# Hybrid diffusion step on one Trainium2 core: recurrence and mixing merged into one block, with the gate-bias wait placed later

## What is computed

```
h   = rmsnorm(x) * (1 + scale1) + shift1                 # modulation from SiLU(c) @ ada_w + ada_b
p   = h @ w_in + b_in                                    # q, k, v, o, 16 gates, 512 Fourier columns
C_loc, n_loc = sum_l w_l v_l k_l^T, sum_l w_l k_l        # per 128-row chunk, 4 heads, 2 directions
C_new = a C + bb C_loc                                   # scan over the chunks: the states
hm  = normalised (intra-chunk part + C_s q), both directions, * head_g * sigmoid(o)
fu  = real(fftn(u)) over (grid rows, grid columns, channels)
x   = x + gate1 * (concat(hm, fu) @ w_out)
h   = rmsnorm(x) ...; x = x + gate2 * ExpertChoiceMoE(h) # 16 experts
```

## Time and profile before

| | us |
|---|---|
| median of 3 runs | 2373.26 (2371.6 to 2374.95) |
| the profiled execution | 2370.94 |
| its span, first to last instruction | 2369.1 |
| input projection, TensorE's first to last L463 | 32.1 to 427.3 |
| recurrence block, SP's first transfer | 437.4 |
| mixing block, SP's first transfer | 519.3 |
| first output product (L1215) | 553.3 |
| first transfer of the expert weights | 766.2 |

### The profile page before, as it was taken

How to read it: one execution, slowest core, us unless ns; L and a number is a source line. 1 busy time by engine, 2 the same in 40 slices (tenths; PEclk the granted TensorE clock), 3 DMA queues, 4 the chain that set the end, 5 groups by cost and what they waited for, 6 DMA issues and landing times. The chain is left out here.

```text
span 2369.1 us, 37037 instructions
## 1 busy us (share of the span) xinstructions
PE 2186.1 (92%) x15013; PEld 1890.2 (80%) x15013; DVE 489.5 (21%) x1246; ACT 358.7 (15%) x1012; POOL 270.0 (11%) x266
## 2 busy tenths in 40 slices
PE   5999999868997299999999999999999999999992
PEld 1445454655553299999999999999999999999992
DVE  0111114247764610011111100110111010101102
ACT  0111112323231011101111111011111110111102
POOL 0000000011211102021021120220210202202102
PEclk8999999999999599999999999999999999999996
DMA  9531010245331777797986976978979769779775
GB/s 377 227 130 62 31 62 22 94 149 200 131 109 58 220 263 213 253 353 222 315 280 238 364 219 246 363 220 294 304 231 355 232 246 363 219 275 327 225 257 178
DMA packets 351601, 528.76 MB, mean 223 GB/s; under 512 B 12996, under 2 KB 292284, under 8 KB 348232
## 3 DMA queue, kind: packets, MB, share of 16 engines
q1 hardware_dynamic: 336456, 509.35, 62.1%
q0 software_dynamic: 15104, 18.88, 3.8%
HBM read 492.23 MB, written 35.95 MB: 223 GB/s over the span
## 5 line engine op out<-in xcount | busy, mean ns | idle before, releaser
L1626 PE MATMUL ps_ab<-xeT,ring 128*128 128x144 f32 x8192 | 1009.0, 286 | 14.7 <-DVE xeT L1671 14.7
L1626 PEld LDWEIGHTS ps_ab<-xeT,ring 128*128 128x128 f32 x8192 | 1007.4, 190 | 14.8 <-issue 14.8
L1639 PE MATMUL ps_yy<-hidT,ring 128*128 128x144 f32 x4096 | 504.4, 286 | 0.0
L1639 PEld LDWEIGHTS ps_yy<-hidT,ring 128*128 128x128 f32 x4096 | 502.8, 190 | 0.0
L463 PE MATMUL ps_p<-w_in_sb,hT 128*128 128x512 f32 x720 | 319.6, 597 | 3.0 <-DMA w_in_sb<-in_w_in 3.0
L1675 DVE TENSOR_TENSOR hidT<-silu,ps_ab 128x144 f32<-128x144 f32 x256 | 77.9, 304 | 886.8 <-ACT silu L1593 821.2
L463 PEld LDWEIGHTS ps_p<-w_in_sb,hT 128*128 128x128 f32 x720 | 135.3, 192 | 157.5 <-issue 156.3
L1572 POOL DMA_INDIRECT stream<-ye,slot_row x64 | 101.0, 1578 | 1216.3 <-DVE ye_p L1686 1201.7
L1593 ACT ACTIVATE silu<-ps_ab 128x144 f32<-128x144 f32 x256 | 74.6, 291 | 909.6 <-PE ps_ab L1626 869.7
L1215 PE MATMUL b_z<-y,mixT 128*128 128x512 f32 x288 | 128.1, 597 | 10.6 <-ACT aff L1149 10.3
L1679 DVE STREAM_TRANSPOSE yS<-yT 128x1024 f32<-128x1024 f32 x16 | 19.9, 1245 | 457.2 <-ACT yT_p L1600 457.2
(11 more groups left out here) (250 smaller groups left out, 1076.5 us busy)
## 6 DMA issues: line engine op xcount, KB each, us to landing
ring<-in_exp_w SPq DMA_DIRECT2D x384, 1024.0 KB, 12.4
y<-in_ada_w SPq DMA_DIRECT2D x22, 1024.0 KB, 8.0
w_in_sb<-in_w_in SPq DMA_DIRECT2D x4, 2048.0 KB, 21.6
kv<-kvo SPq DMA_DIRECT2D x15, 512.0 KB, 5.9
kvo<-pr SPq DMA_DIRECT2D x9, 768.0 KB, 3.3
qkT_dram<-qkT SPq DMA_DIRECT2D x9, 512.0 KB, 4.8
qk<-qkT_dram SPq DMA_DIRECT2D x9, 512.0 KB, 5.0
m_in<-m_lanes SPq DMA_DIRECT2D x9, 512.0 KB, 5.6
```

The lines of the kernel that those rows point to most:

```text
L1626: mm = nc.tensor.matmul(ps_ab[f % 2][:, N * w:N * w + N], unit[:, k, bass.ts(c, P)], xeT[:, k], start=(k == 0), stop=(k == DT - 1))
L1639: mm = nc.tensor.matmul(ps_yy[d % 2][:, 0:N], unit[:, f % 2, bass.ts(d, P)], hT[:, f], start=(f == 0), stop=(f == FT - 1))
```

## The change

Two things are changed.

1. In front, VectorE's wait for the gate biases moves from ahead of tile 0 to just ahead of tile 0's `keep_gates`.
2. The block `recurrence` is gone and its work is in `mixing`. Each transform instruction group now handles a pair (`z_sum(p)`: four matmuls of 256 columns into a full bank, `f_sum(p)`: four of 128 columns; 16 pairs; one copy of 512 columns out of PSUM for a z pair, one for two f pairs). TensorE's order is z 0, the initial states, then eight times a state step and `z_sum(n+1)`, `f_sum(n)`; the pairs z 9 to 12 stand in turn 0, z 13 to 15, the last f and the context transform in turn 1. The state sums have one set of banks and are waited for in thirds. k, v have three buffers. In SP's list the loads of tiles 0 and 1, the head gains and the router stand ahead of the fourth and later k, v loads; w_out's four loads wait for z 3, 7, 11 and 15. ScalarE applies the head gains as it copies mixT (four activations of 128 columns for one of 512) and no longer scales w_out. GpSimd copies the Fourier half of mixT for tile i-1 in turn i, one turn ahead of use. Several tiles of mixing share SBUF with the k, v buffers.

```diff
@@ front, VectorE
                     if only(i, 0):
+                        dve.wait_ge(bg_loaded, 16 * 4)
                         keep_gates()
...
                 keep_h(0, 0)
-                dve.wait_ge(bg_loaded, 16 * 4)
                 dve.wait_ge(g.b_in_loaded, 16)
@@ recurrence goes, mixing takes its work
-def recurrence(nc, g):
...
-    KV = 4
...
+    KV, PAIRS = 3, 16
...
+        lanes_in = ((b_n[0], 0), (b_n[0], 1), (b_n[0], 2), (b_n[1], 0), (b_n[1], 1), (b_n[1], 2), (b_i[0], 0), (b_i[0], 1))
@@ mixing, SP
+                sp.dma_start(c_init[:], g.state_C.rearrange("(r v) k -> v r k", v=HD)).then_inc(start_loaded, 16)
+                sp.dma_start(n_init[:], g.state_n).then_inc(start_loaded, 16)
+                for n in range(KV):
+                    load_kv(n)
                 load(0, 0, True)
                 load(1, 1, True)
...
+                for n in range(KV, TILES - 1):
+                    load_kv(n)
+                sp.wait_ge(end_kept, 3)
...
+                sp.wait_ge(kv_summed, TILES - 1)
                 load_x(0, 0)
                 load_x(1, 1)
                 for n in range(DT // 2):
+                    sp.wait_ge(z_summed, (n + 1) * PAIRS // 4)
                     sp.dma_start(g.w_out_sb[:, 2 * n:2 * n + 2], g.w_out_src[:, 2 * n:2 * n + 2]).then_inc(g.w_out_loaded, 16)
@@ mixing, GpSimd (the eight weigh_kv stand ahead of the turns)
-                    if on(i, 0):
-                        if not below(i, 2):
-                            pool.wait_ge(out_summed, 2 * i - 2)
-                        nc.gpsimd.tensor_copy(mixT[:, par, HEADS:DT], g.fuT[:, :, bass.ts(i, P)]).then_inc(mix_pool, 1)
+                    if on(i, 1):
+                        if below(i, 2):
+                            pool.wait_ge(f_kept, PAIRS // 2 + 1)
+                            pool.wait_ge(kv_summed, TILES - 1)
+                        elif not below(i, 3):
+                            pool.wait_ge(out_summed, 2 * i - 4)
+                        nc.gpsimd.tensor_copy(mixT[:, 1 - par, HEADS:DT], g.fuT[:, :, bass.ts(i - 1, P)]).then_inc(mix_pool, 1)
@@ mixing, ScalarE
+                def keep_z(p):
+                    act.wait_ge(z_summed, p + 1)
+                    if p >= 2:
+                        act.wait_ge(f_summed, p - 1)
+                    did(nc.scalar.activation(z_sb[:, p % 2], b_z[p % 2][:], ACT.Copy), z_kept)
...
-                        did(nc.scalar.activation(mixT[:, 1 - par, 0:HEADS], b_m[:].rearrange("p (h n) -> p h n", n=P), ACT.Copy), mix_act)
+                        for h in range(HEADS):
+                            did(nc.scalar.activation(mixT[:, 1 - par, h], b_m[:, bass.ts(h, P)], ACT.Copy, scale=head_g[:, h:h + 1]),
+                                mix_act if h == HEADS - 1 else None)
@@ mixing, TensorE
+                def z_sum(p):
+                    if p >= 2:
+                        pe.wait_ge(z_kept, p - 1)
+                    for u in range(2):
...
+                def state_sum(n):
+                    pe.wait_ge(wv_fwd, n + 1)
+                    pe.wait_ge(wv_bwd, n + 1)
+                    for r in range(LANES):
+                        bank, at = lane_bank(r)
+                        if n and at == 0:
+                            pe.wait_ge(state_kept, LANES * (n - 1) + min(r + 3, LANES))
...
+                for n in range(TILES - 1):
+                    state_sum(n)
+                    fourier(n + 1)
+                    if n == 1:
+                        turn_end(0)
+                        turn_end(1)
+                    if n == 3:
+                        turn_end(2)
...
+                    fill = (9, 10, 11, 12) if below(i, 1) else (13, 14, 15) if below(i, 2) else ()
                     if on(i, 0):
                         score(i, par, half)
                         inter(i, par, 0)
+                    for p in fill[0:1]:
+                        fourier(p)
...
+                    for p in fill[1:2]:
+                        fourier(p)
                     if on(i, 0):
                         intra(i, par, half, 0)
+                    for p in fill[2:3]:
+                        fourier(p)
+                    if fill == (13, 14, 15):
+                        f_sum(PAIRS - 1)
+                        prompt_sum()
...
                         inter(i, par, 1)
+                        for p in fill[3:4]:
+                            fourier(p)
                         intra(i, par, half, 1)
@@ mixing, VectorE (ahead of the turns)
+                for n in range(TILES - 1):
+                    if n + 1 < TILES - 1:
+                        weigh_kv(n + 1)
+                    dve.wait_ge(kv_summed, n + 1)
...
```

More of the change, by code:

```diff
@@ L1155, in turn @@
                         weigh(i, 1)
+                        for p in fill[2:3]:
+                            fourier(p)
+                        if fill == (13, 14, 15):
+                            keep_f(PAIRS // 2 - 1)
+                            keep_prompt()
                         inter(i, 1)
[L1157 to L1158 removed]
+                    for p in fill[3:4]:
+                        fourier(p)
                     if on(i, 3):
@@ L1216, in project, with prompt_sum, fourier, turn_end @@
                     mm.then_inc(out_summed, 1)
+                def prompt_sum():
+                    pe.wait_ge(z_kept, PAIRS)
+                    for grp in range(4):
+                        for c, basis in ((0, g.dft_chan_r), (1, g.dft_chan_i)):
+                            mm = nc.tensor.matmul(b_z[0][:, bass.ts(grp, P)], basis[:, 0:P], g.y_prompt[:, grp, c], start=(c == 0), stop=(c == 1))
+                    mm.then_inc(f_summed, 1)
+                def fourier(p):
+                    z_sum(p)
+                    if p:
+                        f_sum(p - 1)
+                def state_sum(n):
[5 more added lines that the diff above has]
+                            pe.wait_ge(state_kept, LANES * (n - 1) + min(r + 3, LANES))
+                        d = 1 if n and r >= HEADS else 0
+                        mm = nc.tensor.matmul(bank[:, at:at + VW], kv[:, n % KV, d, bass.ts(r % HEADS, P)], wv[:, n % 2, r], start=True, stop=True)
+                    mm.then_inc(kv_summed, 1)
+                def turn_end(n):
+                    if n == 0:
+                        pe.wait_ge(state_kept, LANES)
+                        pe.wait_ge(init_kept, 4)
+                    if n < 2:
+                        for h in range(HEADS):
+                            mm = nc.tensor.transpose((b_s, b_i[1])[n][:, bass.ts(h, P)], c_end[:, HEADS * n + h, 0:HD], g.ident)
+                    else:
+                        pe.wait_ge(end_kept, 1)
+                        mm = nc.tensor.transpose(b_s[0:LANES, 0:HD], c_end[:, :, HD], g.ident)
+                    mm.then_inc(end_turned, 1)
                 def turn_rows(i):
```

341 lines of the change are left out of this document (146 added, 195 removed).

## The result

| | us |
|---|---|
| changed kernel, median of 4 runs | 2505.47 (2504.51 to 2506.3) |
| kernel before, median of 4 runs beside it | 2374.11 (2371.6 to 2375.61) |
| ratio | 1.055 [1.054, 1.057] |
| span of the changed kernel, profiled | 2503.0 |

The forecast was 2330.3 us, and the kernel became 131 us slower. Everything that the change touches went as predicted, within a few us. The loss stands where nothing was changed, in the experts, so the reader should first see the good part and then the other.

A forecast was written before the change was run, and what follows sets the result against it. TensorE was taken as full in experts and channel transforms, idle in state steps, first mixing turns and a front hole; 17.0 + 32.3 - 6.4 = 42.9 us off gave 2328.0, or 2330.3 against the median; range 2321 to 2345.

The forecast's parts named there:

- the one on the slower side: Mixing's later turns: TensorE's wait for GpSimd's copy grows, deciding from about 6 us in each of eight turns; 2378, chance 0.03.
- all parts: Whole kernel: gains of 17.0 and 32.3 us less a loss of 6.4, together 42.9 us.
- 1, wait in front: Front, tile 0: without the gate biases' wait VectorE adds earlier and block 4 starts at 63.2 instead of 80.18: 17.0 us.
- 2 and 3, to the first product: State steps with turns 0 and 1: transforms fill TensorE's idle time, first output product at 521.0 instead of 553.31: 32.3 us.
- 4, later turns: Turns 3 to 10: ScalarE's four scaled activations and GpSimd's later copy cost 6.4 us, bounds 3 and 11.
- their stall: State steps: TensorE waits 3.5 us for k, v load 3, plus 1.0 for the clock; bounds together 0 and 10.
- bound by transfers: State steps: k, v loads 4 to 7 each come late, with a first stall at its bound; 2344, chance 0.09.
- doubled: Later turns: the wait for GpSimd's copy (1.2 us) is not absorbed by aff's; 2338, chance 0.10.

The follow-up runs named there:

- the place put back: Changed kernel with 26 more instructions (52 fulfilled waits) on TensorE in routing, nothing else: 2329.87 us, ratio 0.982.
- the merged block alone: Changed kernel with the 26 hidden instructions and the gate biases' wait put back ahead of the front's loop: 2347.03 us, ratio 0.989.
- the two edits: Changed kernel with 26 instructions, GpSimd's copies early or GpSimd scaling w_out by the head gains: 182.5 and 182.3 us from first to turn 10's first product.

## Why the prediction was wrong

The step that failed is the one with no number: that what is gained ahead of the experts passes through to the end, because their code is untouched. The code is untouched and its place in TensorE's program isn't. The runs showed in its place that the loop of the experts, moved by 24 instructions against blocks of 256, stands 8.1 us in each of 15 repetitions and runs slow for a while after it: 11.57 us each, 174 in all. The kernel before stood 24 places beyond the changed one's; place 20 is slow and 24 fast, so at most four instructions separated it from the slow stretch, and the change took 24 away. None of the rivals had this; the one on the slower side was a wait inside mixing, and its price of 2378 was the wrong size as well as the wrong place. The chance of 0.94 for faster left nothing for a cause outside the touched blocks.

With the place put back, the sum can be read term by term:

| step | predicted | measured |
|---|---|---|
| all parts | -42.9 us | -41.9 (39 to 47) |
| 1, wait in front | -17.0 | -17.2 at block 4, -14.4 (12 to 20) in time |
| 2 and 3, to the first product | -32.3 | -32.0 (one trace each; the start before scatters by 4.5) |
| 4, later turns | +6.4 | +5.4 to turn 10's first product |

- Part 1: VectorE's 42.01 and block 4 at 62.97 or 63.17 are as worked out from the landings of the earlier trace rows. The term is right.
- Parts 2 and 3: right in sum (31.95 us with the merged block alone, 30.1 in the changed kernel: 46.8 less 16.7), from two errors that partly cancel. The steps and their stall took 429.47 to 467.54, 38.1 us instead of the 40.3 summed, mostly since the load came sooner (a wait of 1.49 for 3.5). Turns 0 and 1 took 467.54 to 506.48, 38.9 instead of 33.4 + 1.75: the last transforms ran at a lowered clock (0.57 granted in 496 to 504 us, after waits of 2.62 and 0.79 us). The context transform's 16 rows took 3.62 us, where the kernel before took 1.95 for them, and f 15's eight 2.07 where f 14's took 1.13. The forecast charged nothing for the clock there.
- Part 4: the first product of each turn, with 26 instructions against before, slips by 2.14 us in turn 3 (predicted 2.1), 1.32 in turn 4 (0.45), 0.44, 0.26, 0.13, 0.25 in turns 5 to 8 (0.45 each), 0.49 in turn 9 (0.5), 0.38 in turn 10 (1.5). The mechanisms were right, as the two edits show by giving it back; the division among the turns was wrong at both ends, turn 4 and turn 10. So was that between the two causes: the forecast gave turns 4 to 8 to the four-part copy alone, and with GpSimd's copies early only 0.9 us of the slip is left up to turn 9.
- Rivals: no step became bound by transfers, and GpSimd's copy was partly absorbed by aff's wait (1.31 us <-POOL in turn 5 and 0.40 left for aff), as the forecast had it, not doubled.

## What to carry to other kernels

Before costing an edit at nothing downstream, look for a long loop of one engine behind it: count its instructions and those ahead of it, and ask whether the edit moves it against the blocks in which the program is fetched. The page shows it in one row: instruction packets that grow with the repetitions of a loop, with idle time "<-issue" at its head. Such a row means a fetch only together with the packets. Some idle instructions in a stretch where the engine waits anyway can put the loop back, here for 176 us; they are a remedy for this build only, and every later edit ahead of the loop has to be looked at again.

## What was not expected of the hardware

A TensorE loop of some 1582 instructions runs with no fetch at all from five of the places tried (-32, -22, 24, 26 and 152, counted from the changed kernel's) and fetches nine blocks again in every repetition from the others (-19 to 20), a stretch of 40 to 45 places out of 256. Between 22 and 19 places fewer the time jumps from 2331.6 to 2470.0 us. The holes cost more than themselves: after the first, of 4.37 us, the granted clock is 0.50, and the 512 rows of that expert take 3.3 us more.
